# Experts of 96 slots: three blocks of 128 rows for four experts in a two-layer f32 trunk

## The chip, the cores and the metric

One core of one Trainium2 chip. The metric is the device time of one launch in microseconds. All matrix work is float32.

## The reference, cut to what matters

Two layers over 1024 tokens of width 1024. Each layer normalizes, projects, runs four mixers (a state-space scan, two kinds of full attention and one with a selection of keys), projects back and adds the residual. Then comes the part that the change touches, a mixture of 32 experts in 4 groups:

```python
g_prob = jax.nn.softmax((h @ w_rg + b_rg).astype(F32), axis=-1)
g_p, g_idx = lax.top_k(g_prob, 1)
e_logits = (h @ w_re + b_re).astype(F32).reshape(t, MOE_GROUPS, MOE_EXPERTS_PER_GROUP)
e_in = jnp.take_along_axis(e_logits, g_idx[:, :, None], axis=1)[:, 0]
e_top, e_loc = lax.top_k(e_in, MOE_TOPK)
...
def expert_block(args):
    xb, e = args
    return (jax.nn.silu(xb @ w_gate[e]) * (xb @ w_up[e])) @ w_down[e]
...
return jax.ops.segment_sum(ys * slot_w[:, None].astype(ys.dtype), slot_tok, num_segments=t)
```

Every token goes to 2 of the 8 experts of its best group, so 2048 assignments fall on 32 experts, 64 on average. An expert has w_gate and w_up of 1024 x 256 and w_down of 256 x 1024, 3 MB together. The result is the same whatever the size of the blocks, if every assignment has a slot. The numbers of tokens per expert are fixed by the inputs.

## The kernel before

The program is written engine by engine (`sp` issues most transfers, `pool` the indirect ones, `pe` the matrix products, `act` and `dve` copy out of PSUM and do the arithmetic). Each engine's order is the order of its code; semaphores join them. A layer is one pass of a hardware loop on every engine.

The expert stage begins once routing has been computed by `dve` (lines 1932 to 2038): for each assignment a rank within its expert, from that a slot, and from the slots a table `idx_i` of the token in each slot, one column per block of 128 rows. Every expert owns one block. Assignments beyond the 128th of an expert go to overflow blocks, which come after the 32 and are run by a loop of OVER = 15 conditional iterations at the end (lines 577 to 586 on `sp`, 658 to 669 on `pool`, 1110 to 1117 on `pe`, and likewise on `act` and `dve`); an iteration without a block does nothing.

For block e, which is expert e:
- `pool` (line 653) gathers the 128 token rows from `h2_dram` into `xg`, two buffers, which are freed when the rows have been turned (`x_turned`).
- `pe` turns them with eight transposes, four into bank 0 (L1051) and four into bank 1 (L1057). `act` and `dve` copy them to `xgT`.
- `gate_up` (L1065): eight f32 products, stationary `xgT` (128 contraction rows, 128 columns, the slots), moving the gate and up weights, 512 columns, into bank 2 or 3.
- `act` takes the Silu of the gate half (L1440), `dve` multiplies it with the up half (L2046).
- `turn_a` (L1072): two transposes of the 256 activations; `dve` copies them (L2050).
- `down` (L1082): for two halves of the output, two products each of 512 moving columns, into banks 6 and 7; `act` and `dve` copy them (L1445, L2055), `sp` stores the block to `ys_dram` (L558).

`pe` runs one block behind itself: gate_up(e), turn_a(e-1), turn_x(e+1), down(e-1). Four experts form a `quad`, one pass of an inner loop, as there are NW = 4 buffers for weights (`Wgu`, `Wd`). `sp` (lines 560 to 569) waits for `gu_done` of block e and loads gate and up of expert e+4 into the same buffer, waits for `dn_done` and loads down, then stores the block. Four experts' weights are loaded before the stage. After it `pool` gathers for each token its two result rows (L674), and `dve` adds them with their weights (L2090).

Elsewhere in the kernel the products are cut in pieces in two places. `pair_values` (L795) makes for two heads a product of 64 stationary columns each, for the PSUM partitions 0 to 63 and 64 to 127. `index_pair` (L933) makes two products of 64 contraction rows each. It alternates with `project_half` (L949 and L952), whose products use all of the array.

Of the kernel before, what the change touches and what calls it, by code (L numbers as in the profile page):

```python
# [40 lines left out]
OVER = N_ASSIGN // P - 1  # L41
BLOCKS = EXPERTS + OVER
# [3 lines left out]
QUADS = EXPERTS // NW  # L46

# [28 lines left out]
def trunk(nc, x_in, positions, norm_mix, w_in, conv_w, conv_b, dt_bias, a_log, ssd_d, ssd_norm,  # L76
# [4 lines left out]
    with ctx:  # L81
# [35 lines left out]
        more_than = sb("more_than", [P, N_ASSIGN // P - 1])  # L117
# [107 lines left out]
        xg_in = [sem("xg_in0"), sem("xg_in1")]  # L225
# [14 lines left out]
        y_out = [sem("y_out0"), sem("y_out1")]  # L240
# [196 lines left out]
        over_f = g(16700, OVER + 1)  # L437
        over_i = g(16720, OVER + 1, dt=I32)
        idx_cur = g(16740, 1, dt=I32)
        xg = g(4096, 2, D)  # L440
        xgT = g(6144, 2, K, P)
        sg = g(8192, 2, FF)
        av = g(8704, 2, FF)
        aT = g(9216, 2, 2, P)
        yb = g(9728, 2, D)
# [4 lines left out]
        def _(sp):  # L450
# [3 lines left out]
            for i in range(T // 2):  # L454
# [7 lines left out]
            sp.dma_start(ys_dram[EXPERTS * P:, :].rearrange("(a p) d -> p a d", p=P),  # L462
                         YT[:, 0:1, :].to_broadcast([P, SLOT_ROWS - EXPERTS, D])).then_inc(setup_dma2, 16)
            layer_end(sp, -1)
            with sp.Fori(0, DEPTH) as l:
# [105 lines left out]

                n_over = sp.value_load(over_i[0:1, 0:1], min_val=0, max_val=OVER)
                with sp.Fori(0, OVER) as j:
                    with sp.If(n_over > j):
                        e = j + EXPERTS
# [6 lines left out]
                        settled(sp, y_out[0], (j + (EXPERTS // 2 + 1)) * 16)  # L582
                for s in range(2):
                    sp.wait_ge(y_out[s], 16 * (EXPERTS // 2))
# [10 lines left out]
        def _(pool):  # L595
# [18 lines left out]
            chain(pool.iota(more_than[:, :], pattern=[[P, N_ASSIGN // P - 1]], base=P, channel_multiplier=0,  # L614
# [8 lines left out]
            with pool.Fori(0, DEPTH) as l:  # L623
# [35 lines left out]
                with pool.Fori(0, OVER) as j:  # L659
                    with pool.If(n_over > j):  # L660
                        e = j + EXPERTS
# [6 lines left out]
                        settled(pool, y_out[0], (j + (EXPERTS // 2 + 1)) * 16)  # L668

                for s in range(2):  # L670
                    pool.wait_ge(y_out[s], 16 * (EXPERTS // 2))
# [15 lines left out]
        def _(pe):  # L687
# [24 lines left out]
            with pe.Fori(0, DEPTH) as l:  # L712
# [362 lines left out]
                def down(e, w, s, n):  # L1075
                    pe.wait_ge(a_taken, e + 1)
                    pe.wait_ge(dn_in[w], 16 * n)
# [11 lines left out]
                def quad_of(q, first=False, last=False):  # L1089

                    for w in range(NW):
                        e, s, nx = q * NW + w, w % 2, q * 2 + ((w + 1) // 2 + 1)
                        gate_up(e, w, s, q + 1)
                        finish = not (first and w == 0)
                        if finish:
                            turn_a(e - 1, 1 - s)
                        if not (last and w == NW - 1):
                            turn_x_lo(e + 1, 1 - s, nx)
                            turn_x_hi(e + 1, 1 - s)
                        if finish:  # L1100
                            down(e - 1, (w - 1) % NW, 1 - s, q + 1 if w else q)
# [5 lines left out]
                turn_a(EXPERTS - 1, 1)  # L1107
                down(EXPERTS - 1, NW - 1, 1, QUADS)

                n_over = pe.value_load(over_i[0:1, 0:1], min_val=0, max_val=OVER)  # L1110
                with pe.Fori(0, OVER) as j:
                    with pe.If(n_over > j):
                        turn_x_lo(j + EXPERTS, 0, j + (EXPERTS // 2 + 1))
                        turn_x_hi(j + EXPERTS, 0)
                        gate_up(j + EXPERTS, 0, 0, j + (QUADS + 1))
                        turn_a(j + EXPERTS, 0)
                        down(j + EXPERTS, 0, 0, j + (QUADS + 1))
# [6 lines left out]
        def _(act):  # L1124
# [45 lines left out]
            with act.Fori(0, DEPTH) as l:  # L1170
# [267 lines left out]
                def gate(e, s):  # L1438
                    act.wait_ge(gu_done, e + 1)
                    act.activation(sg[:, s, :], bank(2 + s)[:, 0:FF], ACT.Silu).then_inc(gate_done, 1)  # L1440
# [8 lines left out]
                def quad_of(q, first=False, last=False):  # L1449
                    for w in range(NW):  # L1450
                        e, s = q * NW + w, w % 2
                        gate(e, s)
                        if not (last and w == NW - 1):
                            take_x(e + 1, 1 - s)
                        if not (first and w == 0):
                            take_y(e - 1, 1 - s, q * 2 + (w - 1) // 2)
# [5 lines left out]
                take_y(EXPERTS - 1, 1, EXPERTS // 2 - 1)  # L1462
# [4 lines left out]
                with act.Fori(0, OVER) as j:  # L1467
                    with act.If(n_over > j):
                        take_x(j + EXPERTS, 0)
                        gate(j + EXPERTS, 0)  # L1470
                        take_y(j + EXPERTS, 0, j + EXPERTS // 2)
# [11 lines left out]
        def _(dve):  # L1483
# [70 lines left out]
            with dve.Fori(0, DEPTH) as l:  # L1554
# [404 lines left out]
                def first_max(vals, n, m, idx, onehot, tmp):  # L1959
# [29 lines left out]
                n_more = N_ASSIGN // P - 1  # L1989
                more = g(12288, EXPERTS, n_more)  # L1990
                chain(dve.tensor_tensor(more, cnt[:, :].unsqueeze(2).to_broadcast([P, EXPERTS, n_more]),
                                        more_than[:, :].unsqueeze(1).to_broadcast([P, EXPERTS, n_more]), ALU.is_gt))
# [12 lines left out]
                chain(dve.tensor_scalar(obase[:, :], obase[:, :], float(P), float((EXPERTS - 1) * P), ALU.mult, ALU.add))  # L2005
                chain(dve.tensor_scalar(base[:, :], iota_e, float(P), None, ALU.mult))
                chain(dve.tensor_tensor(obase[:, :], obase[:, :], base[:, :], ALU.subtract))
                chain(dve.tensor_scalar(cande[:, :, :], rank[:, :, :], float(P), None, ALU.is_ge))
# [35 lines left out]
                def gated(e, s):  # L2044
                    dve.wait_ge(gate_done, e + 1)
                    dve.tensor_tensor(av[:, s, :], sg[:, s, :], bank(2 + s)[:, FF:2 * FF], ALU.mult).then_inc(act_done, 1)  # L2046
# [12 lines left out]
                def quad_of(q, first=False, last=False):  # L2059
                    for w in range(NW):  # L2060
                        e, s = q * NW + w, w % 2
                        if not (first and w == 0):
                            take_a(e - 1, 1 - s)
                        gated(e, s)
                        if not (last and w == NW - 1):
                            take_x(e + 1, 1 - s)
                        if not (first and w == 0):
                            take_y(e - 1, 1 - s, q * 2 + (w - 1) // 2)
# [5 lines left out]
                take_a(EXPERTS - 1, 1)  # L2074
                take_y(EXPERTS - 1, 1, EXPERTS // 2 - 1)

                n_over = dve.value_load(over_i[0:1, 0:1], min_val=0, max_val=OVER)
                with dve.Fori(0, OVER) as j:
                    with dve.If(n_over > j):
                        take_x(j + EXPERTS, 0)  # L2080
                        gated(j + EXPERTS, 0)
                        take_a(j + EXPERTS, 0)
                        take_y(j + EXPERTS, 0, j + EXPERTS // 2)
# [46 lines left out]
```

## Time and profile before

| | |
|---|---|
| median of 3 runs | 2938.73 us (2933.47 to 2940.27) |
| the profiled execution | 2944.05 us |
| its span | 2942.3 us |
| TensorE busy | 2503.1 us, 85% |
| VectorE, ScalarE, GpSimd busy | 1228.1, 908.3, 195.6 us |
| mean rate of the DMA | 126 GB/s, 370.44 MB in all |

The span in 40 slices of 73.6 us, each digit a share in tenths:

```profile
PE   5979999188999959999579899973889997899994
PEclk9989999599999979999779899996999997899996
DMA  6100011301000369999411001121010005699985
GB/s 222 40 29 24 32 35 38 95 2 44 1 1 9 121 254 362 369 361 371 167 59 49 7 24 38 40 81 41 2 44 1 10 22 208 243 357 371 364 305 193
```

The two expert stages are where the DMA row shows 6 to 9: slices 14 to 19 and 34 to 39. PEclk is the clock granted to TensorE in tenths of full speed. Times in the trace are counted from the start of the span, which has layer 0 up to about 1491 us.

### The profile page before, as it was taken

The page shows a single profiled execution, that of the slowest core. Times are in us where ns is not written, and L with a number is a line of the kernel's source. Part 1 is how long each engine was busy: PE and PEld are TensorE (multiplying, and loading weights), DVE is VectorE, ACT ScalarE, POOL GpSimd, SP SyncE. Part 2 cuts the span into 40 slices and gives each one's busy share as a digit, 9 for nine tenths or more (in the row PEclk, how much of TensorE's full clock was granted, in tenths as well). Part 3 has the DMA queues.
Part 4 walks back from the last instruction along what each step waited for, and adds up shares of the span by engine and source line. Part 5 has one row for each costly group of instructions (what it writes and reads, how often), then busy time and mean ns, then how long its engine had stood idle before and what let it go on. Part 6 is the DMA issues. An engine that isn't in the chain of part 4 may idle for free.

```text
span 2942.3 us, 30451 instructions
## 1 busy us (share of the span) xinstructions
PE 2503.1 (85%) x10356; PEld 1423.7 (48%) x10374; DVE 1228.1 (42%) x2854; ACT 908.3 (31%) x1878; POOL 195.6 (7%) x372
## 2 busy tenths in 40 slices
PE   5979999188999959999579899973889997899994
PEld 3464445155664635454335644451556645445452
DVE  4342266885551331111332514768755414211115
ACT  2131266654450201111112214765544401111112
POOL 0000021200000000000200000211000000100002
PEclk9989999599999979999779899996999997899996
DMA  6100011301000369999411001121010005699985
GB/s 222 40 29 24 32 35 38 95 2 44 1 1 9 121 254 362 369 361 371 167 59 49 7 24 38 40 81 41 2 44 1 10 22 208 243 357 371 364 305 193
DMA packets 105455, 370.44 MB, mean 126 GB/s; under 512 B 20754, under 2 KB 39912, under 8 KB 80744
## 3 DMA queue, kind: packets, MB, share of 16 engines
q1 hardware_dynamic: 91500, 318.41, 30.2%
q0 software_dynamic: 13824, 50.34, 4.5%
q8 instruction: 76, 1.25, 0.2%
q14 instruction: 55, 0.45, 0.1%
HBM read 304.42 MB, written 64.30 MB: 125 GB/s over the span
## 4 chain that ended last, share of the span: by engine, by line
PE 75%; DVE 13%; ACT 5%; issue 4%; DMA 1%; POOL 0%; ACTq 0%; DVEq 0%; SPq 0%; POOLq 0%
PE bank L1065 15%; PE bank L732 9%; PE bank L1082 8%; PE bank L1013 8%; PE bank L735 6%; PE bank L766 6%; PE bank L696 5%; PE bank L949 4%; PE bank L952 4%; PE bank L795 4%; PE bank L933 2%; ACT group_arena L1318 2%; PE bank L1026 1%; PE bank L1051 1%; DVE residual L2090 1%
## 5 line engine op out<-in xcount | busy, mean ns | idle before, releaser
L696 PE MATMUL bank<-ident,group_arena 128*128 128x128 f32 (+1 forms) x1200 | 201.1, 308 | 129.1 <-DVE group_arena L1537 59.8
L766 PE MATMUL bank<-group_arena 96*128 96x512 f32 (+7 forms) x384 | 165.7, 531 | 133.9 <-ACTq L1216 125.9
L732 PE MATMUL bank<-w_ring,normed_cols 128*128 128x260 f32 (+2 forms) x768 | 268.0, 511 | 0.6 <-PE bank L735 0.6
L696 PEld LDWEIGHTS bank<-ident,group_arena 128*128 128x128 f32 (+1 forms) x1200 | 149.8, 156 | 190.0 <-issue 96.1
L1082 PE MATMUL bank<-heads_cols,group_arena 128*128 128x512 f32 x512 | 231.8, 595 | 2.8 <-DVE group_arena L2050 2.8
L1065 PE MATMUL bank<-w_ring,group_arena 128*128 128x512 f32 x512 | 229.5, 602 | 3.3 <-issue 1.7
L1065 PE MATMUL bank<-normed_cols,group_arena 128*128 128x512 f32 x512 | 224.9, 592 | 0.0
L1013 PE MATMUL bank<-w_ring,heads_cols 128*128 128x512 f32 x512 | 222.6, 594 | 2.0 <-DVEq L251 2.0
L732 PEld LDWEIGHTS bank<-w_ring,normed_cols 128*128 128x128 f32 x768 | 147.0, 192 | 120.0 <-issue 112.6
L1604 DVE TENSOR_REDUCE softmax_stats<-bank 128x1 f32<-128x128 f32 (+7 forms) x192 | 145.5, 758 | 122.7 <-PE bank L771 105.6
L2050 DVE COPY group_arena<-bank 128x256 f32<-128x256 f32 x64 | 27.2, 425 | 395.3 <-PE bank L1072 395.3
L735 PE MATMUL bank<-normed_cols,w_ring 128*128 128x512 f32 x384 | 170.1, 604 | 15.1 <-DMA w_ring<-in_w_in 14.5
L653 POOL DMA_INDIRECT group_arena<-h_rows,group_arena x64 | 60.4, 944 | 1586.1 <-DVEq L2038 973.0
L1065 PEld LDWEIGHTS bank<-w_ring,group_arena 128*128 128x128 f32 x512 | 98.6, 193 | 127.6 <-issue 125.6
L1065 PEld LDWEIGHTS bank<-normed_cols,group_arena 128*128 128x128 f32 x512 | 97.3, 190 | 122.5 <-issue 122.5
L949 PE MATMUL bank<-w_ring,normed_cols 128*128 128x420 f32 (+1 forms) x512 | 154.5, 454 | 0.6 <-PE bank L952 0.6
L1013 PEld LDWEIGHTS bank<-w_ring,heads_cols 128*128 128x128 f32 x512 | 96.3, 190 | 119.1 <-issue 116.7
L766 PEld LDWEIGHTS bank<-group_arena 128*128 128x128 f32 (+1 forms) x384 | 69.6, 211 | 170.3 <-ACTq L1216 125.7
L1440 ACT ACTIVATE group_arena<-bank 128x256 f32<-128x256 f32 x64 | 24.6, 385 | 406.6 <-PE bank L1065 406.6
L1318 ACT ACTIVATE group_arena<-heads_cols,group_arena 128x896 bf16<-128x896 f32 (+1 forms) x124 | 135.6, 1093 | 41.8 <-DVEq L1806 34.1
L1767 DVE TENSOR_SCALAR_CACHE_REDUCE group_arena<-group_arena 128x384 bf16<-128x384 f32 (+3 forms) x200 | 141.4, 755 | 12.1 <-DVE group_arena L1805 11.0
L1082 PEld LDWEIGHTS bank<-heads_cols,group_arena 128*128 128x128 f32 x512 | 92.2, 190 | 95.4 <-issue 91.8
(326 smaller groups left out, 3479.8 us busy)
## 6 DMA issues: line engine op xcount, KB each, us to landing
heads_cols<-in_expert_w_down SPq DMA_DIRECT2D x64, 1024.0 KB, 9.0
w_ring<-in_expert_w_gate SPq DMA_DIRECT2D x32, 1024.0 KB, 10.0
w_ring<-in_expert_w_up SPq DMA_DIRECT2D x32, 1024.0 KB, 14.5
normed_cols<-in_expert_w_gate SPq DMA_DIRECT2D x32, 1024.0 KB, 10.5
normed_cols<-in_expert_w_up SPq DMA_DIRECT2D x32, 1024.0 KB, 15.1
expert_rows<-group_arena SPq DMA_DIRECT2D x64, 512.0 KB, 9.2
w_ring<-in_w_in SPq DMA_DIRECT2D x6, 2048.0 KB, 8.3
expert_rows<-heads_cols SPq DMA_DIRECT2D x1, 8192.0 KB, 28.7
```

Of the source, the lines that this page charges most:

```text
L696: last = pe.transpose(bank(4 + r % 2)[0:rows, col:col + src.shape[0]], src, ident[0:src.shape[0], 0:src.shape[0]])
L732: m = pe.matmul(proj_bank(n)[:, 0:width], HT[:, k, part * P:(part + 1) * P], w, start=(k == 0), stop=(k == K - 1))
L735: m = pe.matmul(proj_bank(n)[0:width, :], w, HT[:, k, part * HALF:(part + 1) * HALF], start=(k == 0), stop=(k == K - 1))
L766: m = pe.matmul(L[:, c0:c1], a["q"](h, t), a["k"](h, c0, c1), start=True, stop=not (by_choice or diagonal))
L795: pe.matmul(O[i * HD:(i + 1) * HD, pair * P:(pair + 1) * P], KINDS[kind]["v"](h + i, b), pT[:, (u + i) % 2, b * P:(b + 1) * P], start=(b = ...
L949: m = pe.matmul(later_bank(n)[:, 0:width], HT[:, k, part * P:(part + 1) * P], w, start=(k == 0), stop=(k == K - 1))
L1013: m = pe.matmul(bank(n % 4)[:, :], YT[:, k, t * P:(t + 1) * P], WR[:, slot, k, :], start=(k == 0), stop=(k == K - 1))
L1065: m = pe.matmul(bank(2 + s)[:, :], xgT[:, s, k, :], Wgu[w][:, :, k, :], start=(k == 0), stop=(k == K - 1))
L1082: m = pe.matmul(bank(6 + h)[:, :], aT[:, s, k, :], Wd[w][:, k, h * HALF:(h + 1) * HALF], start=(k == 0), stop=(k == 1))
L1318: act.activation(sign_junk[:, 0:w], flipped[t], ACT.Sign, bias=trial_bias[:, t - 2:t - 1], scale=SIGN_SCALE, accum_out=thr[:, 0, t - 2:t - ...
L1604: chain(dve.tensor_reduce(st_[:, u % 4, 0:1], PS[n % 2][:, 0:(t + 1) * P], AX_X, ALU.max))
L1767: chain.go(dve.tensor_scalar(to, src(t), limit(t), 0.0, ALU.is_ge, ALU.add, accum_out=thr[:, 0, t - 2:t - 1]))
```

## The change

An expert has CAP = 96 slots. Four experts, 384 slots, fill three blocks of 128 rows, so 24 blocks (PACKED) hold all 32. A block has rows of two experts, and its products are made in pieces: PIECES lists for each of the three blocks the weight buffer, the first row and the number of rows. In the code, rows of a block are stationary columns of the array. Each piece has its own stationary columns and streams its own expert's weights into its own partitions of the same PSUM bank; for each k the pieces of a block stand one after another. Every expert's 96 rows are two pieces, of 64 and of 32; those of the second and third expert lie in two blocks. Assignments beyond the 96th go to overflow blocks, of one expert each and not cut (WHOLE). OVER is 21.

The buffers `xg`, `xgT`, `sg`, `av`, `aT`, `yb` become three, and gate_up has three banks (2, 3, 5). Block r of a quad needs the weights of the experts in it, so `pe` waits for two experts' loads. `sp` loads into a buffer when the last block that uses it is done. The zero fill of `ys_dram` begins at block 24 and covers 22 blocks instead of 16.

```diff
+CAP = 96
+PACKED = EXPERTS * CAP // P
+MORE = (SEQ - CAP + P - 1) // P
+OVER = N_ASSIGN // (CAP + 1)
+BLOCKS = PACKED + OVER
...
+NB = PACKED // QUADS
+
+PIECES = [[(0, 0, 64), (0, 64, 32), (1, 96, 32)],
+          [(1, 0, 64), (2, 64, 64)],
+          [(2, 0, 32), (3, 32, 32), (3, 64, 64)]]
+WHOLE = [(0, 0, P)]
...
+        gu_bank = (bank(2), bank(3), bank(5))
...
-                with sp.Fori(0, QUADS - 1) as quad:
-                    for w in range(NW):
-                        e = quad * NW + w
+                def quad_of(q, first=False, last=False):
+
+                    e, w0 = q * NB, q * NW
+                    if not last:
                         settled(sp, gu_done, e + 1)
-                        load_gu(e + NW, w)
+                        load_gu(w0 + NW, 0)
+                    if not first:
+                        settled(sp, dn_done, e)
+                        load_dn(w0 + 2, 2)
+                        load_dn(w0 + 3, 3)
+                        store_y(e - 1, 2)
+                    if not last:
+                        settled(sp, gu_done, e + 2)
+                        load_gu(w0 + NW + 1, 1)
                         settled(sp, dn_done, e + 1)
-                        load_dn(e + NW, w)
-                        store_y(e, w % 2)
-                for w in range(NW):
-                    store_y(EXPERTS - NW + w, w % 2)
-
+                        load_dn(w0 + NW, 0)
+                    store_y(e, 0)
+                    if not last:
+                        settled(sp, gu_done, e + 3)
+                        load_gu(w0 + NW + 2, 2)
+                        load_gu(w0 + NW + 3, 3)
+                        settled(sp, dn_done, e + 2)
+                        load_dn(w0 + NW + 1, 1)
+                    store_y(e + 1, 1)
...
-                for e in range(EXPERTS):
-                    s = e % 2
-                    if e >= 2:
-                        pool.wait_ge(x_turned, e - 1)
+                for e in range(PACKED):
+                    s = e % NB
+                    if e >= NB:
+                        pool.wait_ge(x_turned, e - NB + 1)
...
-                def gate_up(e, w, s, n):
+                def gate_up(e, pieces, s, n):
                     pe.wait_ge(x_lo, e + 1)
                     pe.wait_ge(x_hi, e + 1)
-                    pe.wait_ge(gu_in[w], 32 * n)
+                    for w in sorted({w for w, _, _ in pieces}):
+                        pe.wait_ge(gu_in[w], 32 * n)
                     for k in range(K):
-                        m = pe.matmul(bank(2 + s)[:, :], xgT[:, s, k, :], Wgu[w][:, :, k, :], start=(k == 0), stop=(k == K - 1))
+                        for w, at, rows in pieces:
+                            m = pe.matmul(gu_bank[s][at:at + rows, :], xgT[:, s, k, at:at + rows], Wgu[w][:, :, k, :],
+                                          start=(k == 0), stop=(k == K - 1))
                     m.then_inc(gu_done, 1)
...
                     for h in range(2):
                         for k in range(2):
-                            m = pe.matmul(bank(6 + h)[:, :], aT[:, s, k, :], Wd[w][:, k, h * HALF:(h + 1) * HALF],
-                                          start=(k == 0), stop=(k == 1))
+                            for w, at, rows in pieces:
+                                m = pe.matmul(bank(6 + h)[at:at + rows, :], aT[:, s, k, at:at + rows],
+                                              Wd[w][:, k, h * HALF:(h + 1) * HALF], start=(k == 0), stop=(k == 1))
...
-                    for w in range(NW):
-                        e, s, nx = q * NW + w, w % 2, q * 2 + ((w + 1) // 2 + 1)
-                        gate_up(e, w, s, q + 1)
-                        finish = not (first and w == 0)
+                    for r in range(NB):
+                        e, s, behind = q * NB + r, r, (r - 1) % NB
+                        gate_up(e, PIECES[r], s, q + 1)
+                        finish = not (first and r == 0)
...
-                chain(dve.tensor_scalar(cande[:, :, :], rank[:, :, :], float(P), None, ALU.is_ge))
+                chain(dve.tensor_scalar(cande[:, :, :], rank[:, :, :], float(CAP), None, ALU.is_ge))
```

The rest of the diff carries the new counts through the same steps on `act` and `dve`, the overflow loops and the routing's arithmetic.

## Rows read from the trace of the kernel before

**Rows 1.** Costliest groups of the expert stage: operation, count, busy, mean; idle before
```profile
L1082 PE MATMUL bank<-heads_cols,group_arena 128*128 128x512 f32 x512 | 231.8, 595 | 2.8 <-DVE group_arena L2050 2.8
L1065 PE MATMUL bank<-w_ring,group_arena 128*128 128x512 f32 x512 | 229.5, 602 | 3.3 <-issue 1.7
L1065 PE MATMUL bank<-normed_cols,group_arena 128*128 128x512 f32 x512 | 224.9, 592 | 0.0
```

**Rows 2.** The chain in order of time, one expert: start, us, what
```profile
1357.59 3.48 PE bank L1082 x8
1361.08 6.87 PE bank L1065 x16
1367.94 0.23 PE bank L1072 x2
1368.17 0.45 PE bank L1051 x4
1368.62 0.44 PE bank L1057 x4
1369.06 3.44 PE bank L1082 x8
```

**Rows 3.** A window of four experts: PE, PEld, DVE, ACT, POOL busy; PEclk, DMA share, GB/s
```profile
1145.80:1191.50 45.70, 45.70 (x137) 22.84 (x136) 8.54 (x16) 6.32 (x12) 3.76 (x4) 1.00 0.99 361
```

**Rows 4.** Timeline of TensorE, attention values: start, us, engine, line, operation
```profile
2248.17 1.97 PE L795 MATMUL bank<-group_arena 128*64 128x128 f32 x32 [1.37 <-DVE group_arena L1526]
2249.94 0.42 PE L799 MATMUL bank<-ident,softmax_stats 128*64 128x128 f32 x4
```

**Rows 5.** Timeline of TensorE, expert stage, transposes of the full width
```profile
1299.73 0.61 PE L1057 MATMUL bank<-ident,group_arena 128*128 128x128 f32 x4
1300.17 3.64 PE L1082 MATMUL bank<-heads_cols,group_arena 128*128 128x512 f32 x8
```

**Rows 6.** Windows of 40 ns, L933 alone: PE and PEld busy, records running (x)
```profile
1801.74:1801.78 0.04, 0.02 (x2) 0.03 (x2) 1.00 0.00 0
1803.14:1803.18 0.04, 0.04 (x4) 0.00 (x0) 1.00 0.00 0
```

**Rows 7.** Timeline of TensorE, pieces of 64 rows between uncut products
```profile
1801.76 1.99 PE L933 MATMUL bank<-group_arena 64*128 64x512 f32 x8
1803.67 3.09 PE L949 MATMUL bank<-w_ring,normed_cols 128*128 128x420 f32 x8
1806.69 1.99 PE L933 MATMUL bank<-group_arena 64*128 64x512 f32 x8
```

**Rows 8.** DMA issues, window 1070 to 1082, then 1278 to 1324: KB, us to landing
```profile
w_ring<-in_expert_w_up SPq DMA_DIRECT2D x1, 1024.0 KB, 7.6
...
w_ring<-in_expert_w_up SPq DMA_DIRECT2D x2, 1024.0 KB, 14.4
```

**Rows 9.** Timeline of TensorE, the stage's first gate and up product
```profile
1063.17 9.78 PE L1065 MATMUL bank<-w_ring,group_arena 128*128 128x512 f32 x16 [0.83 <-issue]
```

**Rows 10.** Timeline of all engines, end of layer 0's stage
```profile
1430.63 3.70 PE L1082 MATMUL bank<-heads_cols,group_arena 128*128 128x512 f32 x8 [0.89 <-DVE group_arena L2050]
...
1434.37 0.69 DVE L2055 COPY group_arena<-bank 128x512 f32<-128x512 f32 x1 [3.79 <-PE bank L1082]
1438.56 0.94 POOL L674 DMA_INDIRECT w_ring<-expert_rows,group_arena  x1 [45.44 <-DMA expert_rows<-group_arena]
...
1447.23 1.30 DVE L2090 SCALAR_TENSOR_TENSOR residual<-w_ring,group_arena,residual 128x1024 f32<-128x1024 f32 x1 [12.17 <-issue]
```

**Rows 11.** Windows: stores alone, gathers alone, weights alone; columns as in rows 3
```profile
955.00:960.00 5.00, 5.00 (x13) 2.25 (x12) 2.14 (x3) 0.85 (x3) 0.00 (x0) 1.00 0.26 105
1055.00:1060.00 5.00, 0.00 (x0) 0.00 (x0) 0.00 (x0) 0.00 (x0) 2.16 (x2) 0.50 0.41 131
1060.00:1065.00 5.00, 3.80 (x10) 2.41 (x11) 0.69 (x1) 1.88 (x2) 0.94 (x1) 0.50 0.36 111
1035.00:1040.00 5.00, 1.35 (x9) 0.95 (x9) 3.14 (x9) 0.44 (x2) 0.00 (x0) 0.50 1.01 421
```

More of the change, by code:

```diff
@@ L224, in trunk @@
         tile_root = sem("tile_root")
-        xg_in = [sem("xg_in0"), sem("xg_in1")]
+        xg_in = [sem(f"xg_in{i}") for i in range(NB)]
         gu_in = [sem(f"gu_in{i}") for i in range(NW)]
@@ L239, in trunk @@
         y_hi = sem("y_hi")
-        y_out = [sem("y_out0"), sem("y_out1")]
+        y_out = [sem(f"y_out{i}") for i in range(NB)]
         back_in = [sem(f"back_in{t}") for t in range(T)]
@@ L581, in _ @@
                         store_y(e, 0)
-                        settled(sp, y_out[0], (j + (EXPERTS // 2 + 1)) * 16)
-                for s in range(2):
-                    sp.wait_ge(y_out[s], 16 * (EXPERTS // 2))
+                        settled(sp, y_out[0], (j + (QUADS + 1)) * 16)
+                for s in range(NB):
+                    sp.wait_ge(y_out[s], 16 * QUADS)
                 with sp.If(l > DEPTH - 2):
@@ L667, in _ @@
                             in_offset=bass.IndirectOffsetOnAxis(ap=idx_cur, axis=0)).then_inc(xg_in[0], 16)
-                        settled(pool, y_out[0], (j + (EXPERTS // 2 + 1)) * 16)
-                for s in range(2):
-                    pool.wait_ge(y_out[s], 16 * (EXPERTS // 2))
+                        settled(pool, y_out[0], (j + (QUADS + 1)) * 16)
+                for s in range(NB):
+                    pool.wait_ge(y_out[s], 16 * QUADS)
                 for t in range(T):
@@ L1073, in turn_a, with down @@
                     m.then_inc(a_turned, 1)
-                def down(e, w, s, n):
+                def down(e, pieces, s, n):
                     pe.wait_ge(a_taken, e + 1)
-                    pe.wait_ge(dn_in[w], 16 * n)
+                    for w in sorted({w for w, _, _ in pieces}):
+                        pe.wait_ge(dn_in[w], 16 * n)
                     wait_later(pe, y_lo, e)
@@ L1089, in quad_of @@
                 def quad_of(q, first=False, last=False):
-                    for w in range(NW):
-                        e, s, nx = q * NW + w, w % 2, q * 2 + ((w + 1) // 2 + 1)
-                        gate_up(e, w, s, q + 1)
-                        finish = not (first and w == 0)
+                    for r in range(NB):
+                        e, s, behind = q * NB + r, r, (r - 1) % NB
+                        gate_up(e, PIECES[r], s, q + 1)
+                        finish = not (first and r == 0)
                         if finish:
[L1096 to L1099, printed above, removed]
+                            turn_a(e - 1, behind)
+                        if not (last and r == NB - 1):
+                            turn_x_lo(e + 1, (r + 1) % NB, q + (r + 1) // NB + 1)
+                            turn_x_hi(e + 1, (r + 1) % NB)
                         if finish:
-                            down(e - 1, (w - 1) % NW, 1 - s, q + 1 if w else q)
+                            down(e - 1, PIECES[behind], behind, q + 1 if r else q)
                 quad_of(0, first=True)
@@ L1106, in _ @@
                 quad_of(QUADS - 1, last=True)
-                turn_a(EXPERTS - 1, 1)
-                down(EXPERTS - 1, NW - 1, 1, QUADS)
+                turn_a(PACKED - 1, NB - 1)
+                down(PACKED - 1, PIECES[NB - 1], NB - 1, QUADS)
                 n_over = pe.value_load(over_i[0:1, 0:1], min_val=0, max_val=OVER)
@@ L1112, in _ @@
                     with pe.If(n_over > j):
[L1113 to L1117, printed above, removed]
+                        turn_x_lo(j + PACKED, 0, j + (QUADS + 1))
+                        turn_x_hi(j + PACKED, 0)
+                        gate_up(j + PACKED, WHOLE, 0, j + (QUADS + 1))
+                        turn_a(j + PACKED, 0)
+                        down(j + PACKED, WHOLE, 0, j + (QUADS + 1))
                 barrier(pe, PHASE["experts"])
@@ L1449, in quad_of @@
                 def quad_of(q, first=False, last=False):
[L1450 to L1456, printed above, removed]
+                    for r in range(NB):
+                        e = q * NB + r
+                        gate(e, r)
+                        if not (last and r == NB - 1):
+                            take_x(e + 1, (r + 1) % NB)
+                        if not (first and r == 0):
+                            take_y(e - 1, (r - 1) % NB, q if r else q - 1)
                 quad_of(0, first=True)
@@ L1468, in _ @@
                     with act.If(n_over > j):
-                        take_x(j + EXPERTS, 0)
-                        gate(j + EXPERTS, 0)
-                        take_y(j + EXPERTS, 0, j + EXPERTS // 2)
+                        take_x(j + PACKED, 0)
+                        gate(j + PACKED, 0)
+                        take_y(j + PACKED, 0, j + QUADS)
                 barrier(act, PHASE["experts"])
@@ L1987, in _ @@
                 chain(dve.tensor_reduce(cnt[:, :], bank(3)[:, 0:T * EXPERTS].rearrange("p (t e) -> p e t", t=T), AX_X, ALU.add))
[L1989 to L1992, printed above, removed]
+                more = g(12288, EXPERTS, MORE)
+                chain(dve.tensor_tensor(more, cnt[:, :].unsqueeze(2).to_broadcast([P, EXPERTS, MORE]),
+                                        more_than[:, :].unsqueeze(1).to_broadcast([P, EXPERTS, MORE]), ALU.is_gt))
                 chain(dve.tensor_reduce(base[:, :], more, AX_X, ALU.add))
@@ L2059, in quad_of @@
                 def quad_of(q, first=False, last=False):
[L2060 to L2068, printed above, removed]
+                    for r in range(NB):
+                        e, behind = q * NB + r, (r - 1) % NB
+                        if not (first and r == 0):
+                            take_a(e - 1, behind)
+                        gated(e, r)
+                        if not (last and r == NB - 1):
+                            take_x(e + 1, (r + 1) % NB)
+                        if not (first and r == 0):
+                            take_y(e - 1, behind, q if r else q - 1)
                 quad_of(0, first=True)
```

57 lines of the change are left out of this document (30 added, 27 removed).

## The prediction

> **What bounds the kernel now.** I read the costliest groups first: the expert stage's products, gate and up at L1065 and down at L1082, are 1,536 records of 592 to 602 ns [rows 1]. The chain in order of time then shows what one expert costs: 16 records of L1065 in 6.87 us, two transposes at L1072 in 0.23, four at L1051 in 0.45, four at L1057 in 0.44, eight records of L1082 in 3.44 to 3.48, all on TensorE, with no other engine and no transfer between them [rows 2]. The five make 11.43 us an expert (from one L1082 to the next, 1357.59 to 1369.06, it is 11.47). A wide f32 product, which the trace splits into two records, is 6.87 / 8 = 0.859 us, so 0.429 us a record; a record is written as 592 ns because its tail overlaps the next.
>
> The windows over four experts say how tight the rest is: 45.7 us, TensorE busy for all of them at granted clock 1.00 (the 2.4 GHz level), VectorE 8.5, ScalarE 6.3, but the DMA share 0.99 at 361 GB/s [rows 3]. So two resources are full at once: TensorE sets the end, and DMA stands right behind it. The stage is 32 such experts per layer, 64 in all, 64 x 11.43 = 731 us of the profiled span of 2942.3.
>
> **What the change does to the counts.** Four experts (a quad) are packed in three blocks. Each quad has three blocks of ten transposes instead of four; three gathers and three stores instead of four; and the same 12 MB of weights. The products go from 4 x (8 + 4) = 48 wide ones to pieces: three in block 0 (64, 32, 32 columns of the array), two in block 1 (64, 64), three in block 2 (32, 32, 64), each times 12 steps, so 96 products of 512 moving columns. If pieces ran one after another, TensorE would have twice the work; if all pieces of a step ran side by side, three quarters. All depends on this.
>
> **What the trace shows of pieces.** The attention values (L795) are pairs of products with 64 columns each, the two of a pair on the lower and upper half. Their 32 records take 2249.94 - 2248.17 = 1.77 us, 55 ns each [rows 4]. Four full-width transposes with the same 128 moving columns take 1300.17 - 1299.73 = 0.44 us, 110 ns each [rows 5]. So two equal column pieces in f32 run side by side at full rate. The index scores (L933) do the same with pieces of 64 rows: in fine windows two records run at once from the start, and four where a pair passes over to the next [rows 6]. Block 1 (64, 64) thus costs 12 x 0.859 = 10.3 us.
>
> Blocks 0 and 2 mix widths: every step goes from a piece of 64 columns to two of 32 and back. No row has 64 beside 32. The nearest rows are those where the array changes from one cut to another: L933 (64-row pieces) alternates with L949 (uncut, 420 columns). The cycle 1801.76 to 1806.69 is 4.93 us [rows 7]; its work is four record times of 0.429 for eight records in pairs, 1.72, and eight of 0.429 x 420/512 = 0.352, 2.82, together 4.54. The two changes of cut cost 0.39 us, 0.197 each. The uncut run is written as ending at 1803.67 + 3.09 = 1806.76, and the first piece as starting at 1806.69, while inside a run of 512 columns a record starts 0.16 us before the one ahead of it ends (592 ns written, 429 apart). So the next cut waits until the array is all but empty. Bounds for 64 to 32: below, no wait at all (the pieces touch different columns; then all three run side by side); above, 0.25 us a change, somewhat over the row. I take the row, 0.197, and with it that the 64 piece does not run beside the 32s.
>
> The Trainium skill, TensorEngine Tiling (Array Packing), section Tiling Modes, lists 128x64 and 128x32 as different configurations and says that changing the mode, not just the tile, drains the engine. Rows 7 agree with it for 64x128 against 128x128; no row here shows it for 64 against 32.
>
> **The sum for a quad.** A mixed step: 64 alone two record times, the two 32s together two more: 4 x 0.429 = 1.72. Twenty-four mixed steps (12 in each of blocks 0 and 2) are 96 record times, the twelve of block 1 another 24: 120 x 0.429 = 51.5 us. Changes of cut: inside the mixed products 15 + 15 + 7 + 7 = 44, and two per block between products and transposes, 6: 50 x 0.197 = 9.8. Transposes 3 x 1.12 = 3.4. Total 64.7 us against 45.7, so 19.0 a quad, 16 quads: +304 us. Nothing hides it; TensorE is the chain. The DMA falls to 15 MB in 64.7 us, so no load is late: the shortest way from a load's issue to its use, gate and up of the second expert (issued when block 1's product is done, used at the next block 0), is one block and its turns, over 20 us, while the later of such a pair of loads lands in 14.4 us even with the DMA full [rows 8].
>
> **The overflow.** Evaluating the reference's routing on its inputs, the fullest expert of layer 0 has 102 tokens, the next 85; of layer 1 the fullest has 92. Before, with 128 slots, no extra block ran (L1065 has just 2 x 32 x 16 = 1,024 records [rows 1]). Now one runs, in layer 0, with nothing beside it: a fresh load of gate and up (the later of the two lands in 7.6 us with little else under way [rows 8]) behind about 1.5 us of register reads and issue, then the product, 6.87 warm to 9.78 as at the stage's cold start [rows 9], about 1.0 for the Silu and its product, 1.3 for the turn of the activations and TensorE's wait for their copy (two transposes and the 0.89 idle), 3.70 for down, 0.69 for the copy, and for issue and landing of the store 3.5, from the copy's end at 1435.06 to the first gather back at 1438.56 [rows 10]. 1.5 + 7.6 + 6.9 + 1.0 + 1.3 + 3.7 + 0.7 + 3.5 is 26 us warm; cold it is 3 more for the first product and 3 for down, 32. I take 28.
>
> **Small parts.** The empty iterations of the overflow loop go from 15 to 21. VectorE's idle 12.17 us after its last copy [rows 10] holds all 15 of them and ends when the first rows, whose gathers start at 1438.56, have come, so an iteration is under 0.8 us and the six more cost 0 to 5 us a layer; I take 0, since the transfer hides them. The zero fill grows from 8 to 11 MB, at the start, under the layer's projections: 0. The routing's comparisons are 32 x 8 and 21 x 32 elements instead of 32 x 15 and 15 x 32, the slot table 46 columns instead of 48: below 1 us either way. A third buffer lets a gather start a block earlier; no wait for gathers is in the chain of the steady part, so 0. Waits on two experts' weights come before a block instead of one; covered as above. SP's queue keeps each load behind the event that frees its buffer, in the order in which those events come, so none is held up by another.
>
> Sum: 304 + 28 = +332. From the profiled execution's 2944.05 that is 3276; the median shown is 5.3 us lower, so **3270 us**. Own range with changes at 0.15 to 0.25 us (800 of them: -38, +42) and the overflow at 20 to 38: 3215 to 3330.
>
> **Rival A: no wait between 64 and 32, all pieces side by side (faster).** Steps cost 0.859 in every block: 36 x 0.859 = 30.9, transposes 3.4, six changes 1.2: 35.5 us of TensorE a quad. Then DMA decides. Weights alone run at 421 GB/s, so 12.6e6 bytes are 29.9 us; a store is 0.26 of 5 us, 1.3, and a gather (0.41 + 0.36) x 5 / 2 = 1.9 [rows 11]: 29.9 + 3 x 3.2 = 39.5. From the full windows, 15/16 of 45.7 is 42.9. I take 41. It would decide from the point at which TensorE needs less than 41 us a quad. Plainly 16 x 4.7 = 75 us gained; but each layer's first four experts are loaded before the stage starts, so only seven quads pass at 41 and the first near 36, and the last products hide nothing: 5 to 12 us more a layer. About -100 with the overflow's +28: 2866, range 2835 to 2905. For it: the pairs of rows 4 to 6 do run side by side, and pieces in different columns have nothing in common. Against it: rows 7. The Trainium skill, TensorE: Matmul & The Clock Gate, Part 3, gives 2.38x for three pieces of 32 columns; that is no mixture of widths, and no run here shows it.
>
> **Rival B: no wait, but only two records in flight.** All rows show pairs, none three. With each piece costing one record time, a step of three is 3 x 0.429: 96 pieces x 0.429 = 41.2, with transposes and changes 45.8 a quad, what it was. Only the overflow is left: 2966 (2950 to 3010). For it: every concurrency in the trace is of two. Against: nothing suggests a limit at two.
>
> **Rival C: pieces one after another.** 192 record times, 82.4, with transposes and changes 87 us a quad, 41.3 more, 16 times, and the overflow: 3630. Rows 4 exclude it for equal pieces; it needs that 512 columns with their own moving data behave otherwise than 128.
>
> **Rival D: the layout changes nothing** (TensorE's gain lost to DMA stalls exactly): 2940 +/- 6.
>
> **Chances.** Forecast 0.50; A 0.29; B 0.13; C 0.05; D 0.03. A measurement of this kernel tells 0.2%, some 6 us, from no change. Faster 0.30 (A, and an edge of D), same 0.02 (D), slower 0.68. The range must hold the forecast's and A's cases: 2840 to 3330; C and A's tail lie outside. The likeliest one's own range is 3215 to 3330.
>
> **What would show it.** Right: a mixed block's eight steps of L1065's successor take about 16.9 us (8 x 2.11), block 1's 6.9; in fine windows the 64 piece's records run alone, then two at a time; a quad is 65 us with the DMA share near 0.7; TensorE stays at 1.00. Rival A: 6.9 us for all three, a quad of 39 to 43 with TensorE idle for weights and the DMA share at 1.00. Rival B: about 10.3 us for a mixed block. The overflow: one further gate and up product in layer 0 alone, some 28 us from the last packed down to the gathers. The prediction fails if records of a 64 and of a 32 piece overlap in time.

## The result, and the profile after

The changed kernel takes 3222.53 us (median of 4 runs, 3218.77 to 3226.42) against 2939.50 beside it (median of 4 as well): 1.0967 times, 95% interval 1.0946 to 1.0988. That is 283 us slower; 332 were forecast, 3270 us in all. The profiled execution took 3218.77 us, with a span of 3216.9.

The chain of waits of the changed kernel in order of time, over one quad of layer 0 (start, us, what). L1096 is gate and up, L1116 down.

```profile
1175.59 3.58 PE bank L1116 x16
1179.17 15.73 PE bank L1096 x48
1196.23 7.51 PE bank L1116 x23
1204.17 6.87 PE bank L1096 x31
1212.36 7.51 PE bank L1116 x22
1220.30 14.91 PE bank L1096 x46
1236.55 3.58 PE bank L1116 x16
```

The stage still consists of TensorE alone [rows 2]. A quad lasts 1236.55 - 1175.59 = 60.96 us, where four experts took 45.78 on average before (1086.33 to 1418.20 are 29 of them). The 48 records of block 0 take 15.73 us: 32 record times of 0.429 and 15 changes of width, so 0.133 a change, and 1.966 a step on average. Block 1, of two equal pieces, takes 6.87, exactly an uncut product's time (its 32nd record stands before down's last one, where the chain does not count it in). Block 2 takes less than block 0, 14.91 by the chain. Its first two pieces of 32 run beside the last two of the down product before them, as the timeline of TensorE shows:

```profile
1218.25 1.63 PE L1116 MATMUL bank<-heads_cols,group_arena 128*64 128x512 f32 x4
1219.26 0.62 PE L1096 MATMUL bank<-normed_cols,group_arena 128*32 128x512 f32 x2
1219.70 0.60 PE L1116 MATMUL bank<-heads_cols,group_arena 128*32 128x512 f32 x2
```

The pieces of down lie in columns 64 to 127, those of gate and up in columns 0 to 63, and from 1219.34 on four records run at once. That saves two record times, 0.86 us, in each quad.

The window of that quad (PE, PEld, DVE, ACT, POOL busy; PEclk, DMA share, GB/s) answers to rows 3: the DMA has fallen from 0.99 to 0.70, the clock is still the 2.4 GHz level.

```profile
1175.60:1236.55 60.95, 60.95 (x224) 14.96 (x226) 6.41 (x12) 4.72 (x10) 2.81 (x3) 1.00 0.70 258
```

Windows of 40 ns over one mixed step of the changed kernel, L1096's products alone (PE busy, records running as x; then PEclk, DMA share, GB/s), answer to rows 6:

```profile
1179.34:1179.38 0.04, 0.04 (x1) 1.00 0.97 410
...
1179.50:1179.54 0.04, 0.04 (x2) 1.00 1.93 819
...
1179.70:1179.74 0.04, 0.04 (x1) 1.00 0.97 410
...
1179.94:1179.98 0.04, 0.04 (x3) 1.00 0.59 205
...
1180.14:1180.18 0.04, 0.04 (x2) 1.00 0.25 102
...
1180.42:1180.46 0.04, 0.04 (x4) 1.00 0.73 307
```

The reader sees the piece of 64 alone: one record, two where its second record follows its first, one again. Only at 1179.94 do the two pieces of 32 start, for 0.12 us beside the tail of the 64, and then run as a pair. The three pieces lie in columns of their own, and yet the 64 and the pair of 32s take turns. The loads of stationary data show the same (start, us, engine, then what), in the last gate and up product of the layer:

```profile
1534.97 0.19 PEld L1096 LDWEIGHTS bank<-normed_cols,group_arena 128*64 128x64 f32 x2 [0.84 <-issue]
1535.97 0.14 PEld L1096 LDWEIGHTS bank<-normed_cols,group_arena 128*32 128x32 f32 x4 [0.81 <-issue]
```

They come in one burst at each change, never ahead of it. Whether the 0.133 us of a change are the emptying of the array or these loads, no run tells apart.

The overflow block in layer 0, timeline of all engines (start, us, engine, line, operation), answers to rows 10:

```profile
1545.74 8.01 PE L1116 MATMUL bank<-heads_cols,group_arena 128*32 128x512 f32 x24 [0.69 <-DVE group_arena L2083]
...
1557.80 0.38 SPq L551 DMA_DIRECT2D w_ring<-in_expert_w_up  x1
...
1564.55 8.69 PE L1096 MATMUL bank<-w_ring,group_arena 128*128 128x512 f32 x16 [9.71 <-DMA w_ring<-in_expert_w_up]
...
1575.19 3.70 PE L1116 MATMUL bank<-heads_cols,group_arena 128*128 128x512 f32 x8 [0.52 <-DVE group_arena L2083]
...
1579.97 0.37 SPq L568 DMA_DIRECT2D expert_rows<-group_arena  x1
1595.62 0.94 POOL L703 DMA_INDIRECT w_ring<-expert_rows,group_arena  x1 [76.32 <-issue]
```

From the end of the packed blocks at 1553.75 to the first gather back is 41.9 us, where it was 4.2. The last 13 are nobody's work: the store has landed at 1579.97 + 2.67 = 1582.64 by the chain, and GpSimd starts its gather at 1595.62.

### The profile page after: what moved, and what is told of

The parts are those of the page before. It is cut to its first block, busy times and chain, and to the rows that moved or that the text cites. A ratio compares the mean times of both kernels' runs of the same rounds, so it can differ in the third digit from the quotient of the medians.

```text
span 3216.9 us, 33267 instructions
## 1 busy us (share of the span) xinstructions
PE 2751.4 (86%) x11784; PEld 1296.7 (40%) x11784; DVE 1195.7 (37%) x2794; ACT 884.5 (27%) x1833; POOL 180.8 (6%) x358
## 4 chain that ended last, share of the span: by engine, by line
PE 77%; DVE 13%; ACT 5%; issue 4%; DMA 1%; DVEq 0%; POOL 0%; SPq 0%; POOLq 0%; ACTq 0%
PE bank L1096 19%; PE bank L1116 10%; PE bank L761 8%; PE bank L1042 7%; PE bank L764 5%; PE bank L795 5%; PE bank L725 4%; PE bank L978 4%; PE bank L981 3%; PE bank L824 3%; PE bank L962 2%; ACT group_arena L1352 1%; DVE residual L2123 1%; PE bank L1055 1%; DVE group_arena L1571 1%
## 5 line engine op out<-in xcount | busy, mean ns | idle before, releaser
L1096 PE MATMUL bank<-w_ring,group_arena 128*32 128x512 f32 (+2 forms) x1040 | 380.8, 612 | 13.0 <-DMA w_ring<-in_expert_w_up 9.7
L1096 PE MATMUL bank<-normed_cols,group_arena 128*64 128x512 f32 (+1 forms) x1024 | 367.8, 605 | 0.0
L1116 PE MATMUL bank<-heads_cols,group_arena 128*64 128x512 f32 (+1 forms) x1032 | 318.5, 606 | 2.9 <-DVE group_arena L2083 2.9
L795 PE MATMUL bank<-group_arena 96*128 96x512 f32 (+7 forms) x384 | 165.5, 530 | 133.2 <-ACTq L1250 125.9
L1096 PEld LDWEIGHTS bank<-normed_cols,group_arena 128*64 128x64 f32 (+1 forms) x1024 | 77.8, 122 | 262.3 <-issue 262.3
L1096 PEld LDWEIGHTS bank<-w_ring,group_arena 128*32 128x32 f32 (+2 forms) x1040 | 81.8, 124 | 235.6 <-issue 223.7
L1116 PEld LDWEIGHTS bank<-heads_cols,group_arena 128*64 128x64 f32 (+1 forms) x1032 | 61.3, 122 | 222.8 <-issue 213.6
L682 POOL DMA_INDIRECT group_arena<-h_rows,group_arena x48 | 45.4, 945 | 1725.9 <-DVEq L2071 965.7
L2088 DVE COPY group_arena<-bank 128x512 f32<-128x512 f32 x49 | 33.9, 692 | 287.5 <-PE bank L1116 287.5
```

The lines of the kernel that those rows point to most:

```text
L795: m = pe.matmul(L[:, c0:c1], a["q"](h, t), a["k"](h, c0, c1), start=True, stop=not (by_choice or diagonal))
L1096: m = pe.matmul(gu_bank[s][at:at + rows, :], xgT[:, s, k, at:at + rows], Wgu[w][:, :, k, :], start=(k == 0), stop=(k == K - 1))
L1116: m = pe.matmul(bank(6 + h)[at:at + rows, :], aT[:, s, k, at:at + rows], Wd[w][:, k, h * HALF:(h + 1) * HALF], start=(k == 0), stop=(k == 1))
```

## The experiments

**All pieces of 32 columns.** The same blocks, the same slots, only the table of pieces:

```diff
-PIECES = [[(0, 0, 64), (0, 64, 32), (1, 96, 32)],
-          [(1, 0, 64), (2, 64, 64)],
-          [(2, 0, 32), (3, 32, 32), (3, 64, 64)]]
+PIECES = [[(0, 0, 32), (0, 32, 32), (0, 64, 32), (1, 96, 32)],
+          [(1, 0, 32), (1, 32, 32), (2, 64, 32), (2, 96, 32)],
+          [(2, 0, 32), (3, 32, 32), (3, 64, 32), (3, 96, 32)]]
```

> The changed kernel with every piece cut to 32 columns: four pieces of 32 in each block, so the array never goes from 64 to 32. Theory (the array holds pieces of one width at a time, and what costs is the lost side-by-side and the change of width): a step of four pieces takes two record times, 0.859 us, TensorE needs 35 us for four experts and the DMA becomes the bound at 39.5 to 42.9 us; the kernel takes 2850 to 2910 us, faster than before the change. Rival (only two records are ever in flight): a step takes 4 x 0.429 = 1.72 us, four experts 66 us, the kernel 3300 us.

Measured: 2828.99 us, 0.9625 times the kernel before (0.9608 to 0.9642), 394 us less than the changed kernel, with half as many products again. That is 21 us below the range of its own expectation, which had the DMA at 39.5 us a quad or more. The chain over one quad:

```profile
1191.52 17.61 DMA w_ring<-in_expert_w_up
1209.13 0.14 issue
1209.27 7.07 PE bank L1096 x64
1216.35 0.43 PE bank L1104 x2
1216.78 0.45 PE bank L1080 x4
1217.23 0.44 PE bank L1086 x4
1217.67 3.57 PE bank L1116 x32
1221.24 6.91 PE bank L1096 x64
...
1228.87 17.46 DMA w_ring<-in_expert_w_up
```

64 records of four pieces take 6.9 to 7.1 us. Fine windows of L1096 in that kernel show four records at once, eight where they overlap:

```profile
1185.74:1185.78 0.04, 0.04 (x4) 1.00 1.96 819
...
1185.86:1185.90 0.04, 0.04 (x8) 1.00 1.99 819
```

So there is no limit of two in flight, and the mixture of widths was what cost the change its gain. By the starts of their first gate and up products the first two quads of layer 0 take 35.3 to 35.5 us, the third 36.3, and from then on the end is set by a transfer: 37.0 to 37.4, in the chain above 1228.87 - 1191.52 = 37.35 us. The windows of two such quads read

```profile
1191.50:1228.90 37.40, 35.56 (x321) 13.04 (x320) 6.46 (x13) 4.74 (x9) 2.81 (x3) 1.00 1.02 423
1228.90:1266.30 37.40, 35.72 (x322) 13.19 (x322) 6.61 (x14) 4.81 (x10) 2.81 (x3) 1.00 1.02 423
```

**The mixture sorted by width.** The changed kernel with its own pieces and an outer loop over widths, in gate_up and in the same way in down:

```diff
-                    for k in range(K):
-                        for w, at, rows in pieces:
+                    for width in sorted({rows for _, _, rows in pieces}):
+                        for k in range(K):
+                            for w, at, rows in pieces:
+                                if rows == width:
```

> The changed kernel with its own pieces, but in each product all steps of one width first and then all of the other, so 10 changes of cut for four experts instead of 50. Theory (a 64 and a 32 never run together; a change costs 0.125 us, as the changed kernel's steps of 1.966 us say): 120 record times, 51.5 us, transposes 3.4, changes 1.3, together 56.2 us for four experts instead of 60.96; 3222 - 76 = 3146 us. Rival (each piece costs one record time, 41.2 us, and the rest, 16.4 us over 50 changes, is 0.33 us a change): 47.9 us for four experts, 3013 us.

Measured: 3154.47 us, 1.0733 times before (1.0715 to 1.0751), 68 less than the changed kernel where 76 were expected. In its chain a mixed gate and up product reads

```profile
1212.22 14.00 PE bank L1098 x48
1226.23 0.44 PE bank L1106 x2
```

Two record times for the 64s, two for the 32s, eight steps, is 13.74; the 0.26 left are two changes, one at its start, where a down product has ended in 64s, and one in its middle. So the quad has 12 changes and not the 10 that were expected. A quad is 56.7 us (from one block's turn, 1188.43, to the same of the next quad, 1245.14), 4.25 less than 60.96: the order takes 38 changes away, 38 x 0.133 = 5.1, and loses the 0.86 that block 2's first step saved. It helps little: the loss is that 64s and 32s do not share the array. The rival of one record time a piece asked for 47.9 us a quad.

**Two pieces of 64 without packing.** The kernel before, each product cut in two of the same expert:

```diff
-                        m = pe.matmul(bank(2 + s)[:, :], xgT[:, s, k, :], Wgu[w][:, :, k, :], start=(k == 0), stop=(k == K - 1))
+                        for at, rows in ((0, 64), (64, 64)):
+                            m = pe.matmul(bank(2 + s)[at:at + rows, :], xgT[:, s, k, at:at + rows], Wgu[w][:, :, k, :],
+                                          start=(k == 0), stop=(k == K - 1))
```

> The kernel before, unpacked, with each product cut in two pieces of 64 columns of the same expert. Theory: two equal pieces run side by side at no cost, and the two changes of cut per expert (to and from the transposes) cost 0.125 to 0.197 us each: 64 x 0.25 to 0.39 = 16 to 25 us, so 2955 to 2965 us. Rival (a cut costs nothing against uncut products): 2940. Rival (pieces cost by their number): 3600.

Measured: 2961.48 us, 1.0074 (1.0057 to 1.0090). The products are as fast as uncut (6.87 us); the 21 us more are 0.33 us an expert for the two changes at the transposes, 0.17 each on average: the first transposes after the cut take 0.44 instead of 0.23, the down product after them 3.58 instead of 3.44.

**The width changed at each step, nothing lost side by side.** As above, but `for at, rows in (((0, 64), (64, 64)), ((0, 32), (32, 32), (64, 32), (96, 32)))[k % 2]`.

> The kernel before, unpacked, with each product cut by turns in two pieces of 64 columns (even k) and four of 32 (odd k): nothing is lost of the side-by-side, but the width changes at every k, 10 times more per expert than with two 64s throughout. Theory (a change from 64 to 32 or back drains the array and costs 0.125 us): 64 x 10 x 0.125 = 80 us above the kernel cut in 64s (2961), 3041 us. Rival (the cost of the mixture is only the lost side-by-side, 64 and 32 can follow each other freely): 2961 us.

Measured: 3060.03 us, 1.042 (1.0399 to 1.0442). It is 98.5 us above the kernel cut in 64s (102 if each is taken against the kernel before that ran beside it). The expectation counted 10 more changes an expert. There are 11, for down ends in 32s and the next gate and up product starts with 64s: 704 changes, 0.14 us each. The chains of the two kernels, this one and then the one cut in 64s:

```profile
1194.62 8.02 PE bank L1066 x48
1202.64 0.44 PE bank L1074 x2
...
1203.97 4.01 PE bank L1085 x24
```
```profile
1194.71 6.87 PE bank L1066 x32
1201.58 0.44 PE bank L1074 x2
...
1202.90 3.58 PE bank L1085 x16
```

Eight changes are 1.15 us in gate and up, the one at its start included, and three are 0.43 in down: 0.144 each. So a change from 64 to 32 columns costs time by itself, as one from uncut to cut does.

**The mixture without packing.** The kernel before with `((0, 64), (64, 32), (96, 32))` in both products. One run.

> The kernel before, unpacked, with every product cut in pieces of 64, 32 and 32 columns of the same expert. Theory: a step is 1.966 us instead of 0.859 whatever experts the pieces belong to, 12 steps and 64 experts: 64 x 12 x 1.107 = +850 us, with the changes at the transposes 3800 us. Rival (the packing of two experts, its waits or its weights from two buffers have a part in the 1.966): less than 3700 us.

Measured: 3819.68 us against 3800 expected; its gate and up product takes 15.88 us, 1.985 a step. That is 32 record times and 16 changes of 0.134, one more than in the changed kernel's block 0, since here it starts after a 32. Two experts in a block and two buffers of weights have no part in the step's cost.

**The overflow block left out.** The changed kernel with `over_f` multiplied by zero before it is copied to `over_i`.

> The changed kernel with the count of overflow blocks set to zero, so the six assignments beyond the 96th of one expert are left out, and all 21 iterations of the loop are empty. Theory by the trace after: from the last packed down to the first gather back is 41.9 us with the block and 4.2 without, so 3222 - 38 = 3185 us, of which 13 us are the 20 empty iterations that GpSimd goes through after the block. As predicted (28 us for the block alone): 3194 us.

Measured: 3189.35 us, 1.0851 (1.0830 to 1.0871), 33 us less than the changed kernel. It leaves out six assignments, so only its time is read. In its trace the first gather follows the end of the packed blocks by 4.7 us, where it was 41.9; the difference in whole runs is smaller than these 37, within their scatter of some 5. It lies between the two expectations and cannot tell the block from the loop.

**The loop ended at its count.** All pieces of 32, and on all five engines:

```diff
-                with pool.Fori(0, OVER) as j:
-                    with pool.If(n_over > j):
+                with pool.If(n_over > 0):
+                    with pool.Fori(0, n_over) as j:
```

> All pieces of 32 columns, and the overflow loops run to the number of overflow blocks and are skipped where it is zero, instead of 21 conditional iterations. Theory (an empty iteration takes 0.65 us on GpSimd, 20 of them stand behind the block in layer 0, and in layer 1 VectorE comes some 4 us late out of its 21): 2829 - 17 = 2812 us. Rival (the iterations are hidden, as I predicted): 2829 us.

Measured: 2813.49 us, 0.9580 (0.9563 to 0.9597), 15.5 less than with the conditional iterations, or 12 if each is taken against the kernel before that ran beside it; 17 were expected. The timeline around the store of the overflow block:

```profile
1384.98 0.37 SPq L568 DMA_DIRECT2D expert_rows<-group_arena  x1
1388.69 0.94 POOL L703 DMA_INDIRECT w_ring<-expert_rows,group_arena  x1 [47.67 <-issue]
```

3.7 us from store to gather instead of 15.65, so 12 of the 13 us were the 20 empty iterations, 0.6 us each. In layer 1, where all iterations are empty, VectorE's idle time before it adds the first rows falls from 14.92 to 11.31 us. This is the fastest version that was run, 4.2% under the kernel before.

**Fewer bytes.** All pieces of 32, and only half of each expert's up weights is loaded (`[:, 0:K // 2, :]` on both sides of the transfer).

> All pieces of 32 columns, and half of each expert's up weights is not loaded (stale values take their place): 10 of the 12 MB for four experts are left. Theory (with 32-column pieces the DMA is the bound, 37.35 us for four experts at 421 GB/s against 35.5 of TensorE): four experts take 35.5 us and TensorE waits for nothing. Rival (TensorE waits for the order and the latency of the loads, not for bytes, or its own work is 37 us): 37 us stay.

It computes with stale values in place of the rest, and its output goes into the next layer's routing, so only the quad is read. The windows of two quads:

```profile
1190.10:1225.70 35.60, 35.60 (x322) 12.98 (x322) 6.41 (x12) 5.03 (x10) 2.81 (x3) 1.00 0.97 384
1225.70:1261.20 35.50, 35.50 (x323) 12.88 (x322) 6.55 (x13) 4.77 (x10) 2.81 (x3) 1.00 0.98 388
```

TensorE is busy throughout, and by the chain the quad is 1225.71 - 1190.40 = 35.31 us. So the 37.35 of the full version are the bytes: 15 MB, 15.7e6, in 37.35 us is 421 GB/s, what the weights alone moved at [rows 11].

## Why the prediction was right, and where its sizes were off

**The 64 does not run beside the 32s.** Right, and shown in three ways: by the fine windows, by all pieces of 32 (3222 to 2829 us) and by the sorted mixture, which keeps the loss. Taken by the letter, the sign of being wrong ("if records of a 64 and of a 32 piece overlap in time") came true for 0.12 us at each change. But records of one width overlap by 0.16 where one follows the other, and a step of 1.966 us is no step of 0.859.

**The price of a change, 0.197 us.** Too high. Between 64 and 32 it is 0.133 (block 0: 15.73 - 13.74 = 1.99 for 15 changes), 0.134 in the mixture without packing and 0.144 in the alternating cut; at the transposes it is 0.17. The row that I took went from pieces of 64 rows to the uncut array; I took its price over unchanged to another pair of cuts. Why a change in the mixture costs 0.01 us less than one in the alternating cut was not settled.

**The quad, 64.7 us against 60.96.** The sum had 120 record times; block 2's first pieces of 32 run beside down's last ones, so there are 118, 50.7 us. With the transposes' 3.4 that leaves 6.9 us for 50 changes, 0.139 each, where 9.8 stood.

**The stage, +304 us.** 16 x (60.96 - 45.78) = +243. From the first gate and up product to the last packed down the two layers are 242.3 us longer.

**The overflow, +28 us.** By the trace, from the last packed down to the first gather, it is 41.9 - 4.2 = 37.7 longer. The block by itself was well sized: 41.9 less the 13 of the loop is 28.9, against the 28 that stood for this stretch. But 4.2 of the stretch were there before, for a store of its own, and the sum did not take them off. The step that failed is "I take 0, since the transfer hides them", on the empty iterations. I looked at VectorE, whose loop stands beside a transfer. GpSimd's stands behind the block: it waits in the first iteration for the overflow store and then has 20 more to go through, ahead of the gathers. In layer 1, where all 21 are empty, VectorE's 14.92 us of idle time before it adds the first rows (10.84 before) is the loop too, as the 11.31 without it shows; GpSimd's is hidden there.

**The sum.** 242.3 + 37.7 + 4.0 at the end of layer 1 = 284, and the medians differ by 283.0. The spans of the two profiled executions differ by 274.6 only. The stretch from layer 0's first gather back to layer 1's first gate and up product, which the change does not touch, was 8.7 us shorter (1068.7 against 1077.5). The clock explains the larger part. Windows of TensorE in the attention of layer 1, the kernel before and then the changed one (columns as in rows 3):

```profile
2254.00:2274.00 20.00, 19.10 (x118) 12.38 (x115) 6.91 (x27) 6.77 (x25) 0.00 (x0) 0.66 0.01 2
```
```profile
2408.10:2428.10 20.00, 17.71 (x149) 11.56 (x149) 10.10 (x38) 9.09 (x31) 0.00 (x0) 1.00 0.01 2
```

The granted clock of the kernel before was 0.50 there, the 1.2 GHz level, from 2260 to about 2273, after TensorE had been busy for 37 of the 40 us from 2218 to 2258. In the changed kernel and in six of the experiments it stayed at 1.00 at that place. The products around it (L795, 2176.0 to 2340.4; in the changed kernel 2331.0 to 2490.0) took 5.4 us longer in the kernel before. It fits that this profile is of an execution 4.5 us above its median. The other 3 us have no cause that I can name.

**Luck in the range.** The range of 3215 to 3330 held the time, but it was made for changes at 0.15 us or more. At what was measured, the changes take 46 us off the 3270 and the 118 record times 14. The two loops, put at nothing, less the 4.2 us of the store, give some 14 back: 3224. Without them it would be near 3210, outside the range. The mechanism was right; that the time came to lie 48 us from the forecast and not 60 is two errors against each other, and so luck.

**Rival A** was ruled out for the change, but its mechanism is what the all-32 version does, so its sum can be checked: 2866 us, 2835 to 2905, against 2829, 6 us under its range. The step that was off is the DMA's 41 us a quad; it is 37.35. I took the share of 0.99 in rows 3 for a full DMA and scaled the 45.7 us by bytes for the upper end, and priced stores and gathers apart from the weights for the lower. The same mixture of weights, gathers and stores moves at 421 to 423 GB/s when TensorE does not hold it back. At 361 the share showed 0.99, and there was still a sixth to be had. Stores and gathers, priced at 9.6 us a quad, took 7.5 (3 MB of the 15).

**Rival B** (two in flight) is refuted by eight records at once; **rival C** by block 1 and by the two 64s.

## What to carry to other kernels

Cut a product into column pieces only of one width: four of 32 cost as much as an uncut product, two of 64 as well, but 64 with 32 costs twice that, whatever the order (14.00 us sorted, 15.73 in turns, 6.87 uncut). Look at the places where the kernel changes from one cut to another and take their gap as a warning, not as the exact price. A loop over "the most that could be" in conditional iterations costs each of its empty ones on the engine that others wait for, so end it at the count.

## What the runs showed of the hardware

- Pieces of one width run beside each other over the border of two products as well (1219.34 on), with up to eight records written at once.
- Four f32 products of 32 stationary columns and 512 moving ones, each with its own weights and moving data, run at the same time: 16 record times of 0.43 us for 64 records.
- A piece of 64 columns and pieces of 32 take turns, though they lie in columns of their own: four record times a step instead of two.
- A change of the cut costs 0.13 to 0.14 us between 64 and 32 columns and 0.17 between uncut and cut in columns, at the 2.4 GHz level; between uncut and pieces of 64 rows it was 0.197 [rows 7].
- A DMA share of 0.99 in a window is no sign of a full DMA: 361 GB/s and 423 GB/s of the same mixture show 0.99 and 1.02.
- An empty conditional iteration took GpSimd 0.6 us.
